# Moving a modulation product from the first norm into the gate merge, and a broadcast load from ScalarE's queue to SP's

## What is computed

```python
sh1, sc1, gt1, sh2, sc2, gt2 = modulation(cond, w_ada, b_ada)   # silu(cond) @ w_ada + b_ada
h = rms_norm(x, norm1_g) * (1 + sc1) + sh1
(a_b, a_c, a_h, g_q, g_k, g_v, g_r, g_lf, g_lb, t_q, t_k, t_v, m_a, m_b, m_c) = split_cols(h @ w_in)
...                                     # three mixers give y_a, y_b, y_c
z = sigmoid(m_a) * (y_a @ w_branch[0]) + sigmoid(m_b) * (y_b @ w_branch[1]) + sigmoid(m_c) * (y_c @ w_branch[2])
x = x + gt1 * (z @ w_out)
h2 = rms_norm(x, norm2_g) * (1 + sc2) + sh2
x = x + gt2 * hier_moe(h2, ...)
```

## Time and profile before

| | us |
|---|---|
| median of three runs | 2199.62 (2198.98 to 2199.97) |
| the profiled execution | 2205.33 |
| its span, first to last instruction | 2203.5 |
| TensorE busy in it | 1898.1 (86%) |
| VectorE / ScalarE / GpSimd busy | 1098.0 / 673.7 / 623.4 |

### The profile page before, as it was taken

One profiled execution on the slowest core, in us unless ns is written; L12 is line 12 of the kernel. 1 busy time (PEld: TensorE's weight loads), 2 busy tenths in 40 slices (PEclk: granted clock), 3 DMA queues, 4 the chain that ended last, 5 costly groups with the idle time before them and its releaser, 6 DMA issues.

```text
span 2203.5 us, 31294 instructions
## 1 busy us (share of the span) xinstructions
PE 1898.1 (86%) x11778; PEld 1658.1 (75%) x11778; DVE 1098.0 (50%) x1518; ACT 673.7 (31%) x962; POOL 623.4 (28%) x421
## 2 busy tenths in 40 slices
PE   2599999999999996599739999999999999739980
PEld 0399999888899884377518999988889997727760
DVE  0326666444232315688673367654432232358884
ACT  1133331243200002377532332224330000227772
POOL 0243333222355430000124333322224554000001
PEclk7799999999999996799959999999999999759995
DMA  8722222111345354799973222211114534159984
GB/s 269 233 72 59 54 64 55 45 51 51 92 118 146 105 194 163 258 377 375 320 271 98 55 63 63 61 46 45 51 57 120 155 105 182 67 184 344 377 297 172
DMA packets 304193, 325.92 MB, mean 148 GB/s; under 512 B 48400, under 2 KB 246160, under 8 KB 304064
## 3 DMA queue, kind: packets, MB, share of 16 engines
q1 hardware_dynamic: 271456, 237.39, 34.9%
q10 hardware_dynamic: 25120, 59.49, 7.3%
q0 software_dynamic: 7488, 27.27, 3.3%
HBM read 290.17 MB, written 33.91 MB: 147 GB/s over the span
## 4 chain that ended last, share of the span: by engine, by line
PE 73%; DVE 9%; ACT 6%; DMA 4%; issue 4%; DVEq 2%; SPq 1%; ACTq 1%; POOL 0%; PEldq 0%; POOLq 0%
PE ps L1705 44%; PE ps L1719 7%; PE ps L2122 5%; PE ps L1960 3%; ACT w_hi L1081 3%; DVE w_lo L1619 2%; PE ps L1807 2%; PE ps L2113 1%; PE ps L2077 1%; PE ps L1951 1%; DMA modA<-mod_scratch 1%; ACT yo L1098 1%; PE ps L1818 1%; DMA yg<-expert_scratch,pos 1%; PE ps L1828 1%
## 5 line engine op out<-in xcount | busy, mean ns | idle before, releaser
L696 POOL CAST w_hi<-raw 128x1024 fp32r<-128x1024 f32 (+2 forms) x182 | 173.0, 951 | 973.6 <-PE ps L1705 795.4
L1705 PE MATMUL ps<-hT_hi,w_hi 128*128 128x320 f32 (+1 forms) x1760 | 409.9, 314 | 3.8 <-DVE hT_lo L1171 3.8
L698 POOL TENSOR_TENSOR w_lo<-raw,w_hi 128x1024 fp32r<-128x1024 f32 (+2 forms) x182 | 401.0, 2203 | 28.4 <-issue 2.5
L1705 PE MATMUL ps<-hT_lo,w_hi 128*128 128x320 f32 (+1 forms) x1760 | 402.5, 310 | 0.0
L1705 PE MATMUL ps<-hT_hi,w_lo 128*128 128x320 f32 (+1 forms) x1760 | 402.2, 310 | 0.0
L1705 PEld LDWEIGHTS ps<-hT_hi,w_hi 128*128 128x128 f32 (+1 forms) x1760 | 292.7, 188 | 15.5 <-issue 7.6
L1705 PEld LDWEIGHTS ps<-hT_lo,w_hi 128*128 128x128 f32 (+1 forms) x1760 | 294.5, 187 | 1.1
L1705 PEld LDWEIGHTS ps<-hT_hi,w_lo 128*128 128x128 f32 (+1 forms) x1760 | 294.1, 187 | 1.1
L726 POOL DMA_INDIRECT xg<-h_scratch,sidx x32 | 30.2, 943 | 447.0 <-PE ps L2113 266.9
L2122 PE MATMUL ps<-w_hi,xT_hi 128*128 128x512 f32 x256 | 109.7, 429 | 40.0 <-DVE w_lo L1619 40.0
L1036 ACT ACTIVATE sg<-ps 128x640 f32<-128x640 f32 x32 | 22.6, 705 | 336.1 <-PE ps L1705 336.1
(11 more groups left out here) (266 smaller groups left out, 3179.1 us busy)
## 6 DMA issues: line engine op xcount, KB each, us to landing
raw<-in_w_in SPq DMA_DIRECT2D x108, 512.0 KB, 4.1
raw<-in_w_ada SPq DMA_DIRECT2D x96, 512.0 KB, 5.8
raw_more<-in_w_exp_down SPq DMA_DIRECT2D x72, 256.0 KB, 6.8
raw<-in_w_exp_gate SPq DMA_DIRECT2D x68, 256.0 KB, 6.0
raw<-in_w_exp_up SPq DMA_DIRECT2D x68, 256.0 KB, 7.7
expert_scratch<-yo ACTq DMA_DIRECT2D x32, 512.0 KB, 6.1
raw_more<-in_w_exp_gate SPq DMA_DIRECT2D x60, 256.0 KB, 6.3
raw_more<-in_w_exp_up SPq DMA_DIRECT2D x60, 256.0 KB, 8.1
```

What stands on the lines that cost most here:

```text
L696: nc.gpsimd.tensor_copy(w_hi[:, ring, 0:n], raw[:, slot, 0:n])
L698: nc.gpsimd.tensor_tensor(w_lo[:, ring, 0:n], raw[:, slot, 0:n], w_hi[:, ring, 0:n].bitcast(F32), ALU.subtract).then_inc(s_split, 1)
L1705: ins = mm(ps[0:m, 2 * b + c, 0:HT], w[:, k * m:(k + 1) * m], act_pair[h][:, chunk0 + k, HT * c:HT * (c + 1)], start=(k == 0 and i == 0), ...
```

## The change

`layer_items` drops pair 1 from the head of each layer's list. Each step n of the merge now takes two quads, one after mB and one after mC: `merge_quad` deals the sixteen quads of pairs 1 and 2, so that pair 1 is made in n = 0 to 3 and pair 2 in n = 4 to 7. Their banks become 6 and 7. The rows of pair 1 are added after n = 3 and stored by ScalarE in n = 4. In layer 0 the small loads move behind all weights and rows of pair 0. In layer 1 SP waits once for the last `r_lo`, loads modB and modA itself, and then starts its list; ScalarE no longer loads them.

```diff
+def merge_quad(n, i):
+    return 1 + n // (KC // 2), 2 * (n % (KC // 2)) + i
 def layer_items(l):
     items = ada_items(0, 0, range(KC)) + [("rows", 0, 0)] if l == 0 else []
-    items += ada_items(l, 1, range(KC)) + [("rows", l, 1)]
     for u, (what, n) in enumerate(ORDER):
         items.append(("unit", l, u))
-        if what == "mB":
-            items += ada_items(l, 2, [n])
-            if n == KC - 1:
-                items.append(("rows", l, 2))
+        if what in ("mB", "mC"):
+            p, k = merge_quad(n, what == "mC")
+            items += ada_items(l, p, [k])
+            if k == KC - 1:
+                items.append(("rows", l, p))
...
-            return ((0 if l == 0 else 4), 2, 6)[p]
+            return ((0 if l == 0 else 4), 6, 7)[p]
...
+                if l:
+                    sp.wait_ge(r_lo, SET + EXU + done * ROUND_UNITS)
+                    hold(sp)
+                    for dst, b in ((modB, 0), (modA, 1)):
+                        for g in range(2):
+                            sp.dma_start(dst[:, g, :], mod_d[g:g + 1, b, :].broadcast_to([P, D])).then_inc(s_modl, 16)
                 for i, item in enumerate(ITEMS[l]):
                     if i >= RAW:
                         wait_free(ITEMS[l][i - RAW])
-                    elif l:
-                        sp.wait_ge(r_lo, SET + done * ROUND_UNITS + i + 1)
...
-                    if i == RAW - 1:
+                    if i == (2 * KC if l == 0 else RAW - 1):
                         load_small(l)
...
-                    act.wait_ge(r_lo, SET + EXU + before * ROUND_UNITS)
-                    load_mod(modB, 0, s_modl)
-                    load_mod(modA, 1, s_modl)
...
-                store_mod(l, 1)
                 act.wait_ge(s_hT, SET + (l + 1) * TILES)
-                act.wait_ge(s_mst, SET + 32 * (l * ADA_PAIRS + 2))
...
+                        if n == KC // 2 and i == 0:
+                            store_mod(l, 1)
...
-                add_rows(l, 1)
...
-                add_rows(l, 2)
+                    if n % (KC // 2) == KC // 2 - 1:
+                        add_rows(l, 1 + n // (KC // 2))
...
-                while quads < KC:
-                    ada_quad(l, 1, quads)
-                    quads += 1
...
-                pe.wait_ge(s_mrow, SET + l * ADA_PAIRS + 2)
...
-                    ada_quad(l, 2, n)
+                    ada_quad(l, *merge_quad(n, 0))
                     if n:
                         pe.wait_ge(s_sig, SET + g)
                     feature(l, "yB", n, merge_pair(n, 1), yT, nk=4, chunk0=4)
                     if n:
                         pe.wait_ge(s_zm, SET + g)
                     feature(l, "mC", n, merge_pair(n, 2), hT)
+                    ada_quad(l, *merge_quad(n, 1))
```

More of the change, by code:

```diff
@@ L105 @@
 RAW, SPL = 6, 3
-B_BEFORE = ((3, 4, 5, 6, 7), (KC,) * TILES)
 ITEMS = [layer_items(l) for l in range(DEPTH)]
@@ L1159, in norm_tile @@
                 V.tensor_tensor(hbuf[:, t % 2, :], hbuf[:, t % 2, :], modB[:, gl(t), :], ALU.add).then_inc(s_h, 1)
-            V.memset(ps[:, 0, :], 0.0)
-            V.memset(ps[:, 2, :], 0.0).then_inc(s_bank, 1)
+            V.memset(ps[:, 0, :], 0.0).then_inc(s_bank, 1)
             dve.wait_ge(s_const, SET + 32)
@@ L1215, in _ @@
                 V.memset(scanm[:, 0:TOK:CHUNK], 0.0)
-                dve.wait_ge(s_mst, SET + 32 * (l * ADA_PAIRS + 2))
+                dve.wait_ge(s_mst, SET + 32 * (l * ADA_PAIRS + 1))
                 for z in (0, SAMPLE + 1, SAMPLE + 2, TOK + 3):
@@ L1749, in _ @@
                         ada_quad(0, 0, k)
-                quads = 0
                 for t in range(TILES):
-                    while quads < B_BEFORE[l][t]:
-                        ada_quad(l, 1, quads)
-                        quads += 1
                     pe.wait_ge(s_h, SET + l * 2 * TILES + t + 1)
```

## The result

The changed kernel took **2222.17 us** (median of four runs, 2221.15 to 2224.63), against 2199.3 for the kernel before on the same chip (2196.54 to 2199.97). The ratio is 1.0113, 95% interval 1.0096 to 1.0131. Slower was forecast; 22.9 us slower was not, and the time lies above the range. The profiled execution took 2224.63 (span 2222.7), 19.2 more in span than the profiled one of before.

What follows compares the result with a forecast made beforehand. TensorE was taken to bound the kernel, with 73% of the chain that ended last. Terms 18.6 + 2.0 - 5.8 - 8 = +6.8, forecast as +6: 2205.6 us, range 2198 to 2212.

Steps and rivals of the forecast that it cites:

- Quads, +18.6: Merge of both layers: 16 added groups of four matmuls cost 1.16 us each on TensorE, covered by nothing; +18.6 us.
- SP's wait, +2.0 (0 to 4.2): Merge: SP issues mC(4) only after pair 1's rows are added, so TensorE stalls; 1.0 us per layer, +2.0 for both.
- Start of layer 0, -5.8 (-11.5 to 0): Start of layer 0: earlier weights and a faster modA load gain 9.6 us, a slower clock and norm cost 3.8.
- the clock: Start of layer 0: first features and norm slow to layer 1's pace at half clock; +3.8 us (2.5 to 5).
- Start of layer 1, -8: Start of layer 1: the modA wait goes and weighing ends earlier, so the norm starts at 1127.2; -8 us.
- the three terms I set against it: Start of layer 1, costs against the gain: 1.5 us for the store, 2 for the first tile, 2 for slower VectorE operations.
- the unloaded tail: Start of layer 1, best end: first gather to end of weighing as in the kernel's last tail, 26.9 us; gain -13.3.
- The third rival: Start of layer 1: gathers stay loaded, norm starts at 1130.4, gaining only 4.7 us; 2209 us in all, chance 0.13.
- the loaded tail of before: Start of layer 1, costly end: first gather to end of weighing stays 35.5 us, ending at 1130.4; gain only 4.7.
- the signs of being wrong that I had set: Quad under 0.8 us; layer 0's modA load falling to 8 or staying at 15; layer 1's gathers as late as before.

Runs made afterwards that it cites:

- layer 0 alone: The change made in layer 0 only, layer 1 as in the kernel before, against the kernel before: 2203.56 us, ratio 1.0039.

## Why the prediction was wrong

- **Quads, +18.6: right.** 1.17 each, in the changed kernel and with nothing else moved.
- **SP's wait, +2.0 (0 to 4.2): right.** TensorE waited 1.0 for the split of mC(4) in layer 0 and 1.9 in layer 1; with the rows moved there is no wait.
- **The end of the merge, not in the sum: some +4.** I followed pair 1's rows to the slot they would hold, and not pair 2's rows away from the slot they had held. The casts of the earlier trace rows, 2.54 and 0.49, already had the price: the first stands beside a split, the second does not, and what kept a split off the second was an item's place in the list.
- **Start of layer 0, -5.8 (-11.5 to 0): mechanism right, size low.** First cast of the merge -7.5, less one quad of 1.2 that is counted above: -8.7. By the medians of the same traces the first norm operation came 12.9 earlier (9.6 taken), and some 4.7 of that went again between there and the merge (3.8 taken, for the clock). The load of modA fell to 10.31 (12.6 taken).
- **Start of layer 1, -8: wrong in sign.** Stages four and five of the table, +1.1 and +2.0 less a quad: +1.9. The wait for modA did go (4.7 between the weighing and the norm became 0.6), but the three terms I set against it, 1.5 for the store, 2 for the first tile and 2 for VectorE, were far too small. From the last low half to the first gather it took 13.15 instead of 7.68, as the store took 7.56 against 3.66: 5.5 where I took 1.5. From the first gather to the end of the weighing it took 36.35, where the unloaded tail takes 26.92: 9.4 where I took 4. The third rival comes nearest, but not by its mechanism. The gathers did get rid of pair 1's loads (ScalarE reached the fifth tile 22.4 behind the first gather, not 27.6); what ate that up was VectorE, which ended 14.0 behind that instead of 7.8, beside the splits. I let the loaded tail of before be the worst case, though there the splits lay for the most part in the wait that the change removes. Of the signs of being wrong that I had set, this one came: the first gather came later, not earlier, and the first norm operation 36.9 behind it, where I had some 32.
- **The router of layer 1, not in the sum: +6.2 between the medians.** I priced the clock at the two starts and nowhere else. For the changed kernel itself this term is taken over from four kernels derived from it; its one trace does not have it.
- **The pair of traces.** Of the 4.7 that the expert stage of layer 0 seemed to lose when I wrote the expectation for layer 0 alone, 3.0 are the first trace of before.

Put together: 6 was forecast; -3 at layer 0's start, +10 at layer 1's, +4 casts, +6 router, +1 at mC(4) make 24, and 22.9 was measured; that the sum comes so near is in part luck, since traces of one kernel differ by 3 in a stage. The step that failed is the start of layer 1, where the terms for the store, the first tile and VectorE were put at 5.5 and measured 14.9, with two places left out of the sum (the last cast and the router). The range was too narrow because its bounds held only what stood beside the edits.

## To carry to other kernels

An idle stretch that a change removes may be the one in which another engine's work lies without harm: before counting a wait as gain, list what runs in it, and where that goes. A list that deals out slots sets the time of everything behind it, so of a moved item look at the slot that it leaves as well as the one that it takes. And take two traces of the kernel before: stages here moved by 3 us between executions of the same code.

## What the runs showed of the hardware

- **VectorE beside GpSimd.** Not only the cast slows (0.49 to 2.47): operations with two inputs went from 1.23 to 3.21 and from 1.28 to 3.37 beside a split. It goes the other way, too; GpSimd by time, changed kernel, first split of layer 1 (the bracket is its idle time before):

```profile
1117.31 0.86 POOL L706 CAST w_hi<-raw 128x384 fp32r<-128x384 f32 x1
1127.81 1.17 POOL L708 TENSOR_TENSOR w_lo<-raw,w_hi 128x384 fp32r<-128x384 f32 x1 [9.64 <-issue]
```

 While VectorE ran operation behind operation GpSimd stood for 9.64, and then held VectorE up in turn. The Trainium skill (SBUF — State Buffer, Who interferes with whom) names both: an operation with two SBUF inputs contends with GpSimd's reads, and who issues first blocks the other. The traces agree; I had cited that section for the cast alone.
- **One stage, three durations.** The same router stage took 37.4, 40.5 or 43.6 to 43.8, and in the kernel before both of the first two. From the first operation of the out stage to the fall of the clock it took 34.0 to 36.2, for the same instructions. The Trainium skill (TensorE: Matmul & The Clock Gate, Part 1: The HAM clock gate) says that the activity monitor runs free of the kernel, so that the change of clock falls where it may; the traces agree.
- **Stores beside loads.** The last expert store, 0.5 MB, took 2.63 to 3.66 in the two traces of before, 6.13 in the one trace with modA and modB alone beside it, and 6.33 to 8.00 in the five traces with the w_in blocks as well; what the blocks add to it is not told apart from the spread.
